# Retention output normalised token-major: statistics, transposes and state updates in another place and order

## What is computed

```
q, k, v, g_ret, ca, cb, ga, gb = split(rms_norm(x) @ w_in)
s = (q @ k.T) * dmat                      # per chunk and head
o = s @ v + (q @ r) * q_decay             # r: recurrent state, 256 x 512 per head
r = r * chunk_decay + (k * k_decay).T @ v
o = (o - mean(o)) * rsqrt(var(o) + EPS) * ret_gn_gain   # over the 512 values of a head
y_ret = (silu(g_ret) * o) @ w_ret_out
```

## Time and profile before

| | |
|---|---|
| median of three runs | 1619.3 us |
| profiled execution | 1619.7 us |
| its span, first to last instruction | 1617.9 us |
| PE busy | 96% |
| DVE busy | 71% |
| ACT busy | 41% |
| mean granted TensorE clock | 0.989 |

### The profile page before, as it was taken

The page is one execution under the profiler, slowest core; times in us unless marked ns, Lnnn a source line. Parts: engine busy times, 40 slices in busy tenths (PEclk is TensorE's granted clock), DMA queues, the critical chain, the costliest instruction groups (busy, mean ns, idle before and its releaser), DMA issues.

```text
span 1617.9 us, 28181 instructions
## 1 busy us (share of the span) xinstructions
PE 1553.4 (96%) x9984; PEld 1428.5 (88%) x9984; DVE 1145.2 (71%) x1696; ACT 666.0 (41%) x973; POOL 284.8 (18%) x257
## 2 busy tenths in 40 slices
PE   6989999999999999999989999999999999999997
PEld 5987878796899999999979979687779998999997
DVE  7999887887757578654456988779786675555544
ACT  4323434352545454343343335253445544443433
POOL 6971100001110019910000400001020100000000
PEclk9989999999999999999999999999999999999999
DMA  6444846566444524444434556647364442444443
GB/s 250 153 167 142 298 141 250 177 227 222 144 144 144 177 92 156 143 151 161 157 117 163 201 178 226 221 171 278 139 222 155 140 144 84 157 149 150 155 157 115
DMA packets 64562, 275.69 MB, mean 170 GB/s; under 512 B 7232, under 2 KB 7232, under 8 KB 55232
## 3 DMA queue, kind: packets, MB, share of 16 engines
q1 hardware_dynamic: 52560, 192.17, 34.4%
q0 software_dynamic: 11888, 82.04, 14.0%
HBM read 230.30 MB, written 43.89 MB: 169 GB/s over the span
## 4 chain that ended last, share of the span: by engine, by line
PE 79%; DVE 10%; issue 6%; DMA 3%; ACT 2%; DVEq 0%; ACTq 0%; POOL 0%
PE bank L415 23%; PE bank L417 21%; PE bank L416 21%; DVE acc L1080 2%; DVE wlo L1045 2%; PE bank L564 2%; DMA rs_out<-state 1%; PE bank L599 1%; PE bank L581 1%; DMA state<-r_in 1%; DVE state L1111 1%; PE bank L547 1%; PE bank L516 1%; DVE x L1351 1%; PE bank L618 1%
## 5 line engine op out<-in xcount | busy, mean ns | idle before, releaser
L415 PE MATMUL bank<-hhi,whi 128*128 128x320 f32 x2016 | 656.0, 325 | 10.6 <-DVE wlo L1045 8.0
L1045 DVE TENSOR_TENSOR wlo<-wring,whi 128x1024 fp32r<-128x1024 f32 x363 | 479.8, 1326 | 244.5 <-ACT whi L782 190.7
L416 PE MATMUL bank<-hlo,whi 128*128 128x320 f32 x2016 | 625.5, 310 | 0.0
L417 PE MATMUL bank<-hhi,wlo 128*128 128x320 f32 x2016 | 625.4, 310 | 0.0
L415 PEld LDWEIGHTS bank<-hhi,whi 128*128 128x128 f32 x2016 | 380.8, 189 | 72.0 <-issue 59.2
L416 PEld LDWEIGHTS bank<-hlo,whi 128*128 128x128 f32 x2016 | 381.6, 189 | 6.0 <-issue 3.8
L417 PEld LDWEIGHTS bank<-hhi,wlo 128*128 128x128 f32 x2016 | 381.0, 189 | 0.0
L782 ACT ACTIVATE whi<-wring 128x1024 fp32r<-128x1024 f32 x264 | 277.6, 1055 | 231.9 <-PE bank L417 231.5
L1080 DVE SCALAR_TENSOR_TENSOR acc<-up,par,acc 128x256 f32<-128x256 f32 x480 | 228.6, 541 | 0.0
L808 ACT ACTIVATE whi<-wring 128x1024 fp32r<-128x1024 f32 x96 | 101.4, 1056 | 101.9 <-PE bank L417 101.9
L812 ACT ACTIVATE sig<-bank 128x320 f32<-128x320 f32 x92 | 40.3, 438 | 207.0 <-PE bank L417 194.4
(11 more groups left out here) (158 smaller groups left out, 2003.2 us busy)
## 6 DMA issues: line engine op xcount, KB each, us to landing
wring<-w SPq DMA_DIRECT2D x364, 512.0 KB, 3.3
state<-r_in POOLq DMA_DIRECT2D x32, 1024.0 KB, 7.0
rs_out<-state POOLq DMA_DIRECT2D x32, 1024.0 KB, 5.1
rp_out<-pst POOLq DMA_DIRECT2D x8, 512.0 KB, 7.5
us<-c_in POOLq DMA_DIRECT2D x2, 1216.0 KB, 5.7
cs_out<-us POOLq DMA_DIRECT2D x2, 1216.0 KB, 8.4
cp_out<-up POOLq DMA_DIRECT2D x2, 1144.0 KB, 4.6
con<-consts POOLq DMA_DIRECT2D x1, 1420.0 KB, 9.5
```

The lines of the kernel that those rows point to most:

```text
L415: pe.matmul(bank[g][:, 0:T], whi[j][:, k, :], hi, start=start and k == 0, stop=False)
L416: pe.matmul(bank[g][:, 0:T], whi[j][:, k, :], lo, start=False, stop=False)
L417: mm = pe.matmul(bank[g][:, 0:T], wlo[j][:, k, :], hi, start=False, stop=stop and k == n - 1)
L1045: return dve.tensor_tensor(dst, value, hi.bitcast(F32), ALU.subtract)
```

## The change

The output stays token-major until it is normalised. PE's two output products write tokens by 512 values: chunk 0 is one matmul, chunk 1 two, all of 512 columns. ACT copies them to `osb`, and X too, as its third chunk. DVE takes mean and variance with `bn_stats` and `bn_aggr`: chunks 0 and 1 in unit 2, the sample's chunk in unit 5, between its last updates. ACT takes log and exp of the few variances (units 3 and 6), DVE forms the shift -mean*rstd (a wait for ACT, `token_shift`), and ACT normalises `osb` in place with per-token scale and bias. PE transposes the result in four tiles of three transposes at (7,2) to (7,5), three to aux and the fourth to X, and DVE multiplies each with gain and gate straight from there (`gated_output`). The matmuls with ones, `centre`, the squares and `normalise` go.

Beside this, the first query moves from (0,6) to (1,0), the second from (1,3) to (1,5); the update pairs move from steps 0, 2, 4, 6 of unit 1 to 0, 3, 5, 7, and by one step in units 4 and 5. DVE does the first two updates ahead of the split of unit 1. One tap moves from unit 5 to unit 6. In the last stage, gated outputs come ahead of the taps of unit 7, and `glo` of heads 0 to 2 behind them.

```diff
...
-AUX_HEAD, AUX_ACT, AUX_DVE = 31, 9, 22
+RSTDS, RS_CONV, RS_POST, RS_FFN, RS_POST2 = 5, 1, 2, 3, 4
+AUX_HEAD, AUX_ACT, AUX_DVE = 32, 7, 25
...
-HEAD_TAPS = (4, 0, 4, 0, 2, 2, 3, 3, 2, 0, 0, 0)
+HEAD_TAPS = (4, 0, 4, 0, 2, 1, 4, 3, 2, 0, 0, 0)
...
-GB_TAPS = (3, 0, 3, 3, 2, 2, 4, 3)
+GB_TAPS = (3, 0, 3, 3, 2, 1, 5, 3)
...
-QUERY_AT = ((0, 6), (1, 3), (4, 3), (5, 3))
-UPDATE_AT = ((1, 0), (1, 2), (1, 4), (1, 6), (4, 4), (4, 6), (5, 4), (5, 6))
+QUERY_AT = ((1, 0), (1, 5), (4, 3), (5, 3))
+UPDATE_AT = ((1, 0), (1, 3), (1, 5), (1, 7), (4, 3), (4, 5), (5, 3), (5, 5))
 PROMPT_STATE_AT = ((2, 3), (3, 3))
-BACK_AT, MEAN_AT, VAR_AT = (5, 7), (6, 5), (7, 7)
+BACK_AT = ((7, 2), (7, 3), (7, 4), (7, 5))
...
-                for i in range(2):
-                    e = 2 * p + i
...
+                o = aux[(A_P + p) % 3]
+                mm = pe.matmul(o[:, :], stm[:, p * P:(p + 1) * P], vtok[:, 0, :], start=True, stop=(p == 0))
+                if p == 1:
+                    mm = pe.matmul(o[:, :], stm[:, SEQ:SEQ + P], vtok[:, 1, :], start=False, stop=True)
...
-            def late_back(l, hd):
+            def late_back(l, hd, e):
                 H = l * HEADS + hd
-                aux_free(H, A_XT)
-
...
+                pos = A_O + e
+                if e < 3:
+                    aux_free(H, pos)
+                pe.wait_ge(o_normed, H * 3 + 3)
+                o = aux[pos % 3] if e < 3 else X
+                for c in range(2):
+                    pe.transpose(o[:, c * P:(c + 1) * P], osb[:, c, e * P:(e + 1) * P], con[:, C_ID:C_ID + P])
+                tokens = con[:, C_ID:C_ID + P].rearrange("p (i g t) -> p g i t", i=4, g=4)
+                pe.transpose(o[:, SEQ:SEQ + P], osb[:, 2, e * P:(e + 1) * P], tokens).then_inc(aux_done, 1)
...
-            def late_mean(l, hd):
-                H = l * HEADS + hd
...
-            def late_var(l, hd):
-                H = l * HEADS + hd
...
+            def rsqrt_of_tokens(H, n, c, table):
+                if table:
+                    log_exp_table()
+                act.wait_ge(mv_done, H * 2 + (n + 1))
+                act.activation(rs3[:, c], mv[:, c, 1], ACT.Ln, bias=eps[:, 0:1]).then_inc(ln_done, 1)
+                act.wait_ge(ln_done, H * 2 + (n + 1))
+                act.activation(rs3[:, c], rs3[:, c], ACT.Exp, scale=-0.5).then_inc(rs_done, 1)
+            def normalise_tokens(H, n, chunks):
+                act.wait_ge(nm_done, H * 2 + (n + 1))
+                for c in chunks:
+                    act.activation(osb[:, c, :], osb[:, c, :], ACT.Identity, bias=nm3[:, c:c + 1], scale=rs3[:, c:c + 1]).then_inc(o_normed, 1)
+            def late(l, hd, j, table):
                 H = l * HEADS + hd
                 if j == 0:
                     for p in range(2):
                         act.wait_ge(aux_done, H * AUX_HEAD + (A_P + p + 1))
-                        act.activation(oT[:, 2 * p:2 * p + 2, 0:SEQ], aux[(A_P + p) % 3][:, :].rearrange("p (e t) -> p e t", e=2),
-                                       ACT.Copy).then_inc(act_aux, 1)
+                        act.activation(osb[:, p, :], aux[(A_P + p) % 3][:, :], ACT.Copy).then_inc(act_aux, 1)
                 if j in (2, 3):
                     d = j - 2
                     act.wait_ge(aux_done, H * AUX_HEAD + (A_PU + d + 1))
                     act.activation(pst[:, d, :], aux[(A_PU + d) % 3][:, :], ACT.Copy).then_inc(act_aux, 1)
+                if j == 3:
+                    rsqrt_of_tokens(H, 0, slice(0, 2), True)
+                if j == 4:
+                    normalise_tokens(H, 0, range(0, 2))
                 if j == 5:
                     act.wait_ge(stat_done, l * STATS + (hd + (ST_X + 1)))
-                    act.activation(xo[:, :], X[:, :], ACT.Copy).then_inc(stat_read, 1)
-                    act.wait_ge(aux_done, H * AUX_HEAD + (A_XT + 1))
...
+                    act.activation(osb[:, 2, :], X[:, :], ACT.Copy).then_inc(stat_read, 1)
+                if j == 6:
+                    rsqrt_of_tokens(H, 1, slice(2, 3), table)
+                    normalise_tokens(H, 1, range(2, 3))
...
-                    for i in range(QUAD):
+                    for i in range(2 if q == 0 else 0, QUAD):
+                        if j == 5 and i == 2:
+                            token_stats(l, hd, 1, range(2, 3))
+                            dve.wait_ge(bn_done, (l * HEADS + hd) * 3 + 3)
                         update(l, hd, (0, 8, 12)[q] + i)
+                    if j == 5:
+                        token_mean_var(range(2, 3))
...
-            def centre(l, hd):
+            def token_stats(l, hd, n, chunks):
                 H = l * HEADS + hd
-                dve.wait_ge(aux_done, H * AUX_HEAD + (A_MEAN + 1))
-                mean = aux[A_MEAN % 3][:, 0:T].rearrange("p (o t) -> p o t", o=1).to_broadcast([P, 4, T])
...
+                if n == 0:
+                    dve.wait_ge(act_aux, H * AUX_ACT + 5)
+                else:
+                    dve.wait_ge(stat_read, l * STATS + (hd + (ST_X + 1)))
+                for c in chunks:
+                    dve.bn_stats(bn[:, c, :], osb[:, c, :]).then_inc(bn_done, 1)
+            def token_mean_var(chunks):
+                for c in chunks:
+                    mean_var = dve.bn_aggr(mv[:, c, :], bn[:, c, :])
+                mean_var.then_inc(mv_done, 1)
+            def token_shift(l, hd, n, c):
                 H = l * HEADS + hd
-
-                dve.wait_ge(rope_step, (H + (1 if last else 2)) * ROPES)
...
+                dve.wait_ge(mv_done, H * 2 + (n + 1))
+                dve.wait_ge(rs_done, H * 2 + (n + 1))
+                dve.scalar_tensor_tensor(out=nm3[:, c], in0=mv[:, c, 0], scalar=-1.0, in1=rs3[:, c],
+                                         op0=ALU.mult, op1=ALU.mult).then_inc(nm_done, 1)
+            def taps_and_tokens(l, hd, j, n):
+                H = l * HEADS + hd
+                if j == 2:
+                    token_stats(l, hd, 0, range(0, 2))
+                    dve.wait_ge(bn_done, H * 3 + 2)
+                    conv_taps(l, n)
+                    token_mean_var(range(0, 2))
+                else:
+                    if j == 3:
+                        token_shift(l, hd, 0, slice(0, 2))
+                    conv_taps(l, n)
+            def gated_output(l, hd, e):
+                H = l * HEADS + hd
+                pos = A_O + e
                 dve.wait_ge(sg_ready, H * 4 + 4)
-                for e in range(0, 4, 2):
-                    for i in (e, e + 1):
...
+                dve.wait_ge(aux_done, H * AUX_HEAD + (pos + 1))
+                dve.scalar_tensor_tensor(out=go[:, hd * 4 + e, :], in0=(aux[pos % 3] if e < 3 else X)[:, 0:T], scalar=g_(G_RET + hd * 4 + e),
+                                         in1=sg[:, e, :], op0=ALU.mult, op1=ALU.mult).then_inc(dve_aux, 1)
...
+                    if j == 1 and not first:
+                        update(l, hd - 1, 0)
+                        update(l, hd - 1, 1)
+                    if j == 6 and not first:
+                        token_shift(l, hd - 1, 1, slice(2, 3))
                     split(l, U_HEAD + j, hd)
+                    if j == 7 and not first:
+                        for e in range(3):
+                            gated_output(l, hd - 1, e)
+                    if j == 8 and not first:
+                        gated_output(l, hd - 1, 3)
                     if not first:
                         updates(l, hd - 1, j)
-                    conv_taps(l, taps[j])
+                        taps_and_tokens(l, hd - 1, j, taps[j])
+                    else:
+                        conv_taps(l, taps[j])
                     if j == 1 or j == 3:
                         rope(l, hd, j // 2, first)
-                    if j == 6 and not first:
-                        centre(l, hd - 1)
                     if j == 9:
                         decayed_keys(l, hd)
                         masked_scores(l, hd)
-                        if not first:
-                            normalise(l, hd - 1)
...
+                    if n == 1:
+                        update(l, last, 0)
+                        update(l, last, 1)
+                    if n == 6:
+                        token_shift(l, last, 1, slice(2, 3))
                     split(l, U_GB + n)
                     updates(l, last, n)
-                    conv_taps(l, GB_TAPS[n])
-                    if n == 6:
-                        centre(l, last)
                     if n == 7:
-                        dve.wait_ge(pst_stored, l * (HEADS * 16) + HEADS * 16)
-                        for s in range(2):
...
+                        dve.wait_ge(sample_conv_step, (l + 1) * SAMPLE_OPS)
+                        for e in range(4):
+                            gated_output(l, last, e)
+                    taps_and_tokens(l, last, n, GB_TAPS[n])
+                dve.wait_ge(pst_stored, l * (HEADS * 16) + HEADS * 16)
+                dve.wait_ge(r_stored[0], l * (HEADS * 32) + HEADS * 32)
+                gated_low(0)
```

(3 more changed lines are left out.)

103 lines of the change are left out of this document (23 added, 80 removed).

## The result

| | before | after |
|---|---|---|
| median (range) | 1620.3 us (1619.0 to 1623.8), 6 runs | 1611.4 us (1607.4 to 1621.1), 6 runs |
| ratio to before | | 0.9948 (0.9930 to 0.9966) |
| profiled execution | 1619.7 us | 1621.1 us, the longest of its six |
| its span, mean granted clock | 1617.9 us, 0.989 | 1619.3 us, 0.977 |

The change gains 8.9 us, where 22 were forecast. 1611.4 lies above 1606, the end of the range. The profiled execution of after happens to be its longest; the other five have spans of 1605.6 to 1611.3 us and clocks of 0.980 to 0.984. So what ate the gain shows there at its largest, and not at its usual size.

A forecast was written before the change was run, and what follows sets the result against it. PE, 96% busy, was taken to set the pace. Six middle heads (-20.4 us) and the last stages (-1.9) made -22.3 from the profiled 1619.7, which is 0.4 above the median: 1597.4, stated as 1597.3 us, range 1589 to 1606.

The forecast's parts named there:

- PE's work: Late heads: two products with ones go (-4.30 us), four transposes become twelve (+0.87), net -3.4 us a head.
- Unit 1: Late heads, unit 1: no wait at (1,3), a wait of 1.3 us at (1,7), a lead of 0.7 us.
- Units 2 to 5: Late heads: statistics, log and exp delay update 8; PE waits 0.9 us at (4,5), 1.15 in last stages; lead spent.
- the rival by which each switch costs double: ACT table switches in late heads and last stages each cost 1.38 us more: 1614 us, chance 0.04.
- The tail of the last stage: End of last stage: PE waits about 4 us for `glo`; -3.0 and -2.3 us by layer, before 1.7 each for clock.
- The load at (5,3): Query at (5,3) in late heads: the load lands about 0.3 us earlier; heads with this wait gain 0.3, others 0.
- the charge for the clock: Last stages, behind the `glo` wait: one fall to 1.2 GHz in each layer, charged 1.7 us each.
- The rival of 1607: Clock falls behind (1,7) in each late head: 6x1.7 less 2 already there, +8 to +10 us; 1607 us, chance 0.12.
- The likeliest case: Whole kernel: middle heads -20.4 us, last stages -1.9, for 1597.3 us; by itself 1592 to 1603, chance 0.66.

The follow-up runs named there:

- rp_late: Changed kernel with the store of the prompt's state issued behind the loads for the next head, except in last stages: 1598.7 us, 0.9862 to before.
- rp_fill: Changed kernel with the prompt-state store behind the next head's loads and extra PE products (5 at (1,7), 4 at (4,5), 15 ahead of `glo`): 1591.8 us, 0.9819.
- rp_glo_fill: Changed kernel with the late prompt-state store, unit 7's last-stage taps behind `glo`, extra products (5 at (1,7), 4 at (4,5), 5 ahead of `glo`): 1587.8 us, 0.9802.
- fill_no_load: Changed kernel with extra PE products at its stops: 5 at (1,7), 4 at (4,5), 15 ahead of `glo`, none at (5,3): 1599.6 us, 0.9867.
- after_again: The changed kernel, unedited, run again beside others on one chip; its trace is the second one of that kernel: 1611.5 us, 0.9945 to before.

## Why the prediction missed, step by step

**PE's work: right.** -4.30 and +0.87 a head. Undisturbed heads have 67.3 in three kernels (rp_late, rp_fill, rp_glo_fill), for 67.5.

**Unit 1: right.** 1.47 for 1.3 at (1,7), none at (1,3).

**Units 2 to 5: right.** 1.04 for 0.9 at (4,5); 1.24 for 1.15 in last stages. The prices that no row of the kernel before showed, on DVE (after the bar the total in us, the mean in ns and the idle time ahead):

```profile
L1118 DVE BATCH_NORM_STATS2 bn<-osb 128x6 f32<-128x512 f32 x24 | 15.7, 684 | 0.0
L1123 DVE BATCH_NORM_AGGREGATE mv<-bn 128x2 f32<-128x6 f32 x24 | 3.4, 168 | 0.0
```

and on ACT in unit 3 of the last stage:

```profile
384.49 1.28 ACT L769 ACT_TABLE_LOAD   x1
385.78 0.29 ACT L801 ACTIVATE rs<-mv,eps 128x2 f32<-128x2 f32 x1
386.11 0.20 ACT L803 ACTIVATE rs<-rs 128x2 f32<-128x2 f32 x1
386.33 1.28 ACT L794 ACT_TABLE_LOAD   x1
```

0.68 for 0.65, 0.17 for 0.15, 0.29 and 0.20 for 0.25 each, and four more loads in all (33 for 29), two a layer. The log begins 1.29 after the load's start, so the rival by which each switch costs double is dead: the drain that the Trainium skill, page "ScalarE: Activation LUTs", section "What ACT_TABLE_LOAD costs", adds to a switch doesn't show in this kernel either.

**The tail of the last stage: right in place, too cheap in clock.** 3.78 for about 4, `osb` 0.85 for 0.8. The fall of the clock was charged 1.7 a layer, the smaller of the two losses in the earlier trace rows; it begins inside the wait and runs to 422.2, so some 2.8 of work are lost on PE behind it. The same stage has two more falls, behind its (1,7) and (4,5) waits; before it had one in layer 0 and none in layer 1.

**The load at (5,3): wrong.** The working said that a head with this wait gains 0.3 and one without gains 0. It took the load times of before as given (6.2 us in five of eight heads). After, six of eight took 9.3 to 10.1, and the waits grew by 7.5. In the second trace they are 1.8 against 3.1 and didn't grow. It varies from one execution to the next, so what this step costs the median isn't shown; the rest, of which it is a part, misses its forecast by 2.0 us.

**The step that failed: the charge for the clock.** The sum had 3.4 for it, one fall in each last stage, and the falls in the heads were a rival with a chance of 0.12 at 1607, though the earlier trace rows showed a stop of 1.12 followed by a fall in some heads. The chance for at least some falls was near one: a 1.47 brings one in two to five of eight heads in each trace with that stop. And the rival stopped at the two update waits of the middle heads; it left out the load waits (20.4 of the 54.6 us at 1.2 GHz in the first trace, 3.4 of 30.7 in the second) and the update waits of the last stages. The likeliest case should have been the sum with such falls in it. Measured in means, the clock took 13.8 us for the 3.4 charged, and all else gave 23.7 for 25.7. The rival of 1607, with its chance of 0.12, named the right mechanism, and 1611.4 lies beyond even that; the upper end of 1606 was too near.

**What stays open.** Why the load takes 6.2 in one head and 9.4 in the next. Moving the store of the prompt's state shortens it to 6.1 to 8.0, so that transfer has a part in it; the rest wasn't separated from weights and the other stores. Nor did any run test why the same stop brings a fall in one head and not in the next.

## What to carry to other kernels

When PE sets the pace and loses work, price the clock in the likeliest case: list every stop that is left or made longer, also the waits for transfers, and take the share of like stops followed by a fall in the trace. A stop that can't be removed may be filled: some products whose result nobody reads, for a little less than the wait, gave 0.8% here (fill_no_load against after_again). When PE comes earlier to a query, look at once for the transfer that it will now wait for, and at what is queued beside it.
